# 320 bytes of padding in front of the activation tiles of a two-block fp32 transformer kernel

## What is computed

```python
for i in range(2):                       # first_block
    h = rms_norm(x, g[0])
    h = mlstm_mixer(h, ...) if i == 0 else short_conv_mixer(h, ...)
    x = x + rms_norm(h, g[1])
    h = sqrelu_mlp(rms_norm(x, g[2]), w_mlp_up[i], w_mlp_down[i])   # 1024 -> 4096 -> 1024
    x = x + rms_norm(h, g[3])
# second_block
x = x + concatenate([y_ret, y_pool]) @ w_out
x = x + cross_attn(rmsnorm(x, xa_norm_g), mem_n, wq, wkv, wo)
x = x + conv_glu_ffn(rmsnorm(x, ffn_norm_g), w_up, conv_w, conv_b, w_down)   # 1024 -> 2 x 2816, 2816 -> 1024
return rmsnorm(x, final_norm_g)

def sqrelu_mlp(x, w_up, w_down):
    h = jax.nn.relu(x @ w_up)
    return (h * h) @ w_down
```

## The kernel before

| tile | address before | modulo 512 |
|---|---|---|
| raw0, wH0, wL0, x | 16,512, 49,280, 65,664, 82,048 | 128 |
| xnH, xnL, memH, memL | 91,712, 99,904, 108,096, 116,288 | 64 |
| ident, ones, y, squares, hrelu0, hsq0 | 140,864, 141,376, 144,960, 153,152, 144,960, 149,056 | 64 |
| hH and mixH, hL, mixL | 161,344, 194,112, 169,536 | 64 |
| xpn0, hn0 | 185,920, 181,888 | 64, 128 |

## Time and profile before

### The profile page before, as it was taken

How to read it: one execution, slowest core, us unless ns; L and a number is a source line. 1 busy time by engine, 2 the same in 40 slices (tenths; PEclk the granted TensorE clock), 3 DMA queues, 4 the chain that set the end, 5 groups by cost and what they waited for, 6 DMA issues and landing times.

```text
span 996.5 us, 20181 instructions
## 1 busy us (share of the span) xinstructions
PE 960.1 (96%) x8062; PEld 946.0 (95%) x8062; DVE 660.3 (66%) x843; ACT 534.8 (54%) x754; POOL 186.4 (19%) x159
## 2 busy tenths in 40 slices
PE   8999989999999899989999999889999999999995
PEld 7999989999999799989999999889999999999995
DVE  6667586665444877678665444774775779999642
ACT  5566646654444545556655443545554566666541
POOL 2121140000000400149100010455120122222101
PEclk9999999999999999999999999999999999999998
DMA  8533635555555355535655554544443545555521
GB/s 341 191 127 120 218 127 192 191 174 206 173 197 180 112 197 199 179 129 201 211 179 201 207 174 154 205 145 164 139 158 105 178 142 179 200 181 198 210 87 43
DMA packets 25844, 172.17 MB, mean 173 GB/s; under 512 B 3252, under 2 KB 3892, under 8 KB 5432
## 3 DMA queue, kind: packets, MB, share of 16 engines
q1 hardware_dynamic: 25784, 171.30, 49.5%
HBM read 170.24 MB, written 1.05 MB: 172 GB/s over the span
## 4 chain that ended last, share of the span: by engine, by line
PE 63%; DVE 15%; issue 6%; POOL 2%; ACT 2%; DVEq 1%; ACTq 0%; POOLq 0%
PE po L404 19%; PE po L405 19%; PE po L406 19%; DVE wL L1230 7%; DVE xnL L1237 2%; POOL rtok L1806 2%; DVE cval L1741 1%; DVE cgate L1741 1%; DVE apad L1728 1%; ACT wH L790 1%; PE po L432 1%; PE po L433 1%; PE po L431 1%; PE pn L479 1%; PE pc L728 1%
## 5 line engine op out<-in xcount | busy, mean ns | idle before, releaser
L1230 DVE TENSOR_TENSOR wL<-raw,wH 128x1024 fp32r<-128x1024 f32 x318 | 411.7, 1318 | 157.7 <-ACT wH L790 157.3
L790 ACT ACTIVATE wH<-raw 128x1024 fp32r<-128x1024 f32 x318 | 332.3, 1057 | 255.7 <-PE po L406 226.7
L404 PE MATMUL po<-xnH,wH 128*128 128x256 f32 x1376 | 391.4, 284 | 18.9 <-DVE xnL L1237 13.4
L405 PE MATMUL po<-xnL,wH 128*128 128x256 f32 x1376 | 383.6, 279 | 0.0
L406 PE MATMUL po<-xnH,wL 128*128 128x256 f32 x1376 | 383.4, 279 | 0.0
L404 PEld LDWEIGHTS po<-xnH,wH 128*128 128x128 f32 x1376 | 259.2, 188 | 24.3 <-DVE xnL L1237 10.3
L405 PEld LDWEIGHTS po<-xnL,wH 128*128 128x128 f32 x1376 | 260.5, 189 | 0.2
L406 PEld LDWEIGHTS po<-xnH,wL 128*128 128x128 f32 x1376 | 260.0, 189 | 0.0
L404 PE MATMUL po<-hH,wH 128*128 128x256 f32 x688 | 191.4, 278 | 1.3 <-DVE wL L1230 1.3
L405 PE MATMUL po<-hL,wH 128*128 128x256 f32 x688 | 191.3, 278 | 0.0
L406 PE MATMUL po<-hH,wL 128*128 128x256 f32 x688 | 191.3, 278 | 0.0
(11 more groups left out here) (284 smaller groups left out, 1083.8 us busy)
## 6 DMA issues: line engine op xcount, KB each, us to landing
raw<-in_weights SPq DMA_DIRECT2D x158, 1024.0 KB, 4.8
x<-in_xT SPq DMA_DIRECT2D x4, 256.0 KB, 5.7
raw<-in_weights SPq DMA_DIRECT2D x2, 512.0 KB, 5.5
mem<-in_memT SPq DMA_DIRECT2D x1, 1024.0 KB, 13.1
out<-y SPq DMA_DIRECT2D x4, 256.0 KB, 2.4
decayt<-in_decay SPq DMA_DIRECT2D x1, 512.0 KB, 3.7
poolwt<-in_poolw SPq DMA_DIRECT2D x1, 256.0 KB, 3.6
par<-in_params SPq DMA_DIRECT2D x1, 164.0 KB, 3.4
```

The lines of the kernel that those rows point to most:

```text
L404: pe.matmul(psum[:, n, 0:T], wH[w][:, wc], aH[:, ac, :], start=start, stop=False)
L405: pe.matmul(psum[:, n, 0:T], wH[w][:, wc], aL[:, ac, :], start=False, stop=False)
L790: act.activation(wH[b % HL][:, hs], raw[b % RAW][:, hs], ACT.Copy).then_inc(s_hi, 1)
L1230: dve.tensor_tensor(wL[b % HL][:, hs], raw[b % RAW][:, hs], wH[b % HL][:, hs].bitcast(f32), ALU.subtract)\
```

## The change

```diff
@@ -102,6 +102,7 @@
         minus_half = sb("minus_half", [P, 2 * NH], f32)
         rtok = sb("rtok", [P, TT], f32)
         rmem = sb("rmem", [P, TT], f32)
+        gap = sb("gap", [P, 80], f32)
         xnH = sb("xnH", [P, C, T], f32r)
         xnL = sb("xnL", [P, C, T], f32r)
         memH = sb("memH", [P, C, T], f32r)
```

## The result

The changed kernel takes 1027.97 us (median of 4 runs, 1027.05 to 1029.74), the kernel before 998.3 in the same comparison. The ratio is 1.029 with a 95% interval of 1.025 to 1.034. The profiled execution takes 1029.74 us, with a span of 1027.4, 30.9 us longer than the span of before.

What follows compares the result with a forecast made beforehand. The prediction took TensorE's matmul spacing and stream breaks to bound the kernel. Adding 0 + 0 + 0 to the profiled 998.9 us, with a spacing draw centred there and on 1000.3, gave 999 us, range 982 to 1018.

Steps and rivals of the forecast that it cites:

- the first term of the sum: Spacing of the 7,632 weight-slab matmuls on TensorE: a distance of 256 bytes was priced at 0.
- the shares of the prediction: Slab matmuls split by spacing: 2,166 long and 2,702 short in the windows, plus 1,382 of the rest to each.
- The crossings: Places where the stream passes unbroken between moving tiles 64 above and 64 below the loaded ones: either spacing claimed unchanged.
- the transposes: Products with ident moving: 0.11 us between starts with hn loaded (64 bytes off) and with xpn (same place modulo 512).
- B: Rival: the offset holds the slab matmul stream at the long spacing, 18.0 us more, 1016.9 us; chance 13%.
- D: Rival: the offset adds a third, longer spacing to the slab matmuls, 33.6 us beyond B, 1050.5 us; chance 5%.
- The two squares of ScalarE: Squares of 128x512 from hrelu and from x, 618 and 619 ns at different tile places: moved tiles were priced at nothing.
- the store of y: Last DMA store, the only one on the path among moved tiles: 2.4 us to landing, a tenth would be 0.2 us.
- the runs of before differ by their two spacings: Runs 993.19 to 1001.28 us, 8.1 us apart, read as 1,840 matmuls changing spacing between executions.
- the spacing is picked where the stream breaks: TensorE's matmul stream was said to fall into 113.3 or 117.8 ns after a break and keep it until the next.

Runs made afterwards that it cites:

- e2_all_moved: The 320 bytes of padding put in front of raw, so every tile moves and the distance stays 64 bytes, against the kernel before: 1001.29 us, ratio 1.000.
- e3_gap64: The changed kernel with 64 bytes of padding in place of 320, moving tiles at distance 0 from the weight tiles: 1027.71 us, ratio 1.028 to the kernel before.
- e4_gap_hidden: The 320 bytes put behind the first region, so only hH, hL, mixH, mixL and the mixers' tiles move, against the kernel before: 1013.6 us, ratio 1.014.
- e6_gap128: The changed kernel with 128 bytes of padding in place of 320, moving tiles 64 bytes above the weights: 1010.59 us, ratio 1.009 to the kernel before.
- e1_sweep: Separate kernel without the network, streaming runs of 48 matmuls at 24 tile places, other engines idle: 113.5 to 120.0 ns per matmul at weights 0.
- e5_fine: Separate kernel without the network, runs of 48 matmuls with the moving tile at 16-byte steps and finer, after four kinds of break: nothing shorter than 113.3 ns.
- e8_d112: Moving tiles 112 bytes above the weights modulo 256, par and five small tiles moved behind memL, against the kernel before: 994.78 us, ratio 0.996.
- e10_pattern: Separate kernel without the network: the slabs' three-product pattern at several distances, roles turned, and ten wait lengths at 192: eight waits gave 5.73 us runs, two 5.92.
- e9_d192: The layout of e8_d112 but at the distance of the kernel before, 192 modulo 256: 994.79 us, ratio 0.995 to the kernel before.
- e11_fp32_moved: Kernel before with only memk and everything behind it moved to where e9_d192 has it, by 224 and 32 bytes of padding: 995.0 us, ratio 0.997.

## Why the prediction was wrong

**The step that failed is the first term of the sum**, the price of the new distance for the 7,632 matmuls. I bounded it by 0, +64 and -64 bytes, saw no difference and took 0. It is 120.0 ns: 2.2 more than the long spacing and 6.7 more than the short one. With the shares of the prediction (3,548 matmuls long, 4,084 short) that is 7.8 + 27.4 = 35.2 us; TensorE's busy time grew by 33.6 us, and its idle time shrank by 2.7 (36.4 to 33.7 us): 30.9 us of span. Here e2_all_moved, e3_gap64 and e4_gap_hidden show the cause: all tiles moved together cost nothing, distance 0 by another padding costs the same, and with only hH, hL, mixH, mixL and the mixers' tiles moved it is 1013.6 us.

**Why the evidence misled.** The crossings compare +64 with -64, and e6_gap128 shows that these two share both spacings, so they said nothing of 256. Nor do they hold for every crossing. In the same trace, at 623 us, the stream passes from the one to the other without a break:

```profile
622.39 0.28 PE L431 MATMUL po<-wH,memH 128*128 128x256 f32 x1
...
623.45 0.29 PE L404 MATMUL po<-memH,wH 128*128 128x256 f32 x1
...
623.69 0.28 PE L406 MATMUL po<-memH,wL 128*128 128x256 f32 x1
...
624.71 0.28 PE L406 MATMUL po<-memH,wL 128*128 128x256 f32 x1
```

Nine matmuls in 1.06 us are 117.8 ns, and nine in 1.02 us are 113.3 ns. So "leaves either spacing as it was" was wrong: a change of the pair alone can swap the spacing. These rows of before were a sign that the place matters, and the prediction left them out. A distance of 0 was among the transposes, with xpn loaded, and showed no extra; but they are another kind of product, and a slab's matmul at distance 0 takes 120.0 ns, as e3_gap64 shows. I also took "the trace has no other pair" as a reason to stay at zero, where it was a reason to stay open.

**The Trainium skill** says in SBUF — State Buffer, "Who interferes with whom", that TensorE's moving operand and its weight load have independent read ports and that TensorE waits on nobody. The prediction concluded that an offset between the two can be worth nothing. The runs contradict that conclusion: the place of the one relative to the other moves the spacing from 113.3 to 120.0 ns, with all other engines still (e1_sweep). The formula N / 2.4 + 2.5 in TensorE: Matmul & The Clock Gate, "Back-to-back issue gap", gives 109.2 ns for 256 columns; the page means an isolated matmul by it, not one in a stream of weight loads and matmuls. In the streams here no distance reached it, the least is 113.3. That SBUF has 16-byte lines (SBUF — State Buffer, "Specifications (TRN2)") fits the runs: places off the 16-byte grid settled at 119.0 ns or more (e5_fine). But 0, 80 and 96, on the grid, are at 120.0 as well, and no run shows that the lines are the reason.

**The rivals.** What came is between B and D: no stretch keeps the short spacing, as in B (1016.9 us), and a third, longer one takes its place, as in D (1050.5). D had the right kind and a step of 4.4 ns where 2.2 came; with 2.2, its own working gives 1016.9 + 7,632 x 2.2 ns = 1033.7 us, 4 above the profiled execution. Its chance was 5%, and the range ended at 1018.

**What held.** The two squares of ScalarE got no longer (616 and 618 ns), and the store of y stayed at 2.4 us. That the runs of before differ by their two spacings fits, but is argued: they span 993 to 1012 us beside the experiments, while the changed kernel, which has one spacing, stays within 1027.05 and 1029.74, and e8_d112, with 113.3 in the ordinary slabs, within 992.46 and 996.88. That the spacing is picked where the stream breaks is shown by e10_pattern; that it changes only there is wrong, as the crossing at 623 us and e4_gap_hidden show.

**Open:** what inside TensorE or SBUF makes the 16-byte steps and the period of 256 bytes. The runs show the table, not the circuit. Also open is what makes e9_d192 faster than the kernel before at the same distance, and whether it is the place of the tiles behind memL (e11_fp32_moved leaves that undecided).

## What to carry to other kernels

In a stream of float32r matmuls of this shape that each load weights, the address of the moving tile less that of the loaded one, modulo 256 bytes, is a knob worth up to 6% of the matmul time (113.3 against 120.0 ns); other types and shapes were not tried. Read the distance of starts, not the length of a matmul, and try a few distances in a stream of 48, with the real pattern of tiles, before padding anything. Keep operands on 16 bytes, and avoid equal addresses modulo 256. Where a kernel's runs spread by a per cent, look for stretches of the same code at two spacings.

## What the runs showed of the hardware that was not expected

- The spacing of float32r matmuls (128 weight columns, 256 moving columns, clock 1.00) depends on the distance of the two tiles modulo 256 bytes: 120.0 ns at 0, 80 and 96, 116.7 or 117.8 at 32, 113.3 or 117.8 at 64 and 192, 113.3 at 112, 118.5 to 120.0 at 128, 119.0 to 121.5 off the 16-byte grid. With the roles of the tiles turned, 144 gave 120 instead of 116.7 or 118.8 (e10_pattern).
- At 64 and 192 two spacings, 113.3 and 117.8 ns, are stable over 1,400 matmuls and more; at 192 a wait that is 0.03 us longer can swap them (e10_pattern).
- A new distance shows with the first matmuls, and in full after some nine (113.5, then 118, then 120 ns in e4_gap_hidden).
